# A mixture-of-experts stage: from pairs of experts with 64 sorted slots to fours of experts with 32 tokens each

## The reference

```python
group_p = softmax(xt @ w_group);  group_w, group_id = top_k(group_p, 1)
in_group = (xt @ w_router) restricted to that group
top_logits, local_id = top_k(in_group, 2)
gates = group_w * softmax(top_logits)
# per expert e, over its tokens:
h = silu(xb @ w_gate[e]) * (xb @ w_up[e]);  y_e = h @ w_down[e]
y[token] += gate * y_e          # two experts per token
```

## Time and profile before

| | |
|---|---|
| time, median of three runs | 3320.39 us |
| the profiled execution's span | 3318.3 us |
| PE busy | 2797.8 us (84%) |
| DVE, ACT busy | 855.7, 472.3 us |
| read from HBM | 777.00 MB, mean 235 GB/s |
| experts, block 1, each of two layers | 237.3 us from first product to last combine |
| experts, block 2, each of two layers | 465.6 us |
| routing, each of four layers | 36.5 to 38.3 us |

### The profile page before, as it was taken

How to read it: one execution, slowest core, us unless ns; L and a number is a source line. 1 busy time by engine, 2 the same in 40 slices (tenths; PEclk the granted TensorE clock), 3 DMA queues, 4 the chain that set the end, 5 groups by cost and what they waited for, 6 DMA issues and landing times. The chain is left out here.

```text
span 3318.3 us, 34187 instructions
## 1 busy us (share of the span) xinstructions
PE 2797.8 (84%) x13108; PEld 1699.9 (51%) x13108; DVE 855.7 (26%) x1849; ACT 472.3 (14%) x879; POOL 0.2 (0%) x4
## 2 busy tenths in 40 slices
PE   6869997868996994869898889869858797988886
PEld 4544445544443852858743333347547686333333
DVE  1442221343122126351121111111364312110111
ACT  1311110321111002200111011010121001101111
POOL 0000000000000000000000000000000000000000
PEclk9889998888998997969989999989978798999998
DMA  6015995114994553003349999864700032899994
GB/s 266 32 54 215 428 419 217 51 46 166 427 428 189 236 192 163 1 1 129 150 191 429 428 429 428 374 276 166 289 1 1 26 152 105 368 429 429 428 429 206
DMA packets 55690, 779.39 MB, mean 235 GB/s; under 512 B 6825, under 2 KB 7081, under 8 KB 7849
## 3 DMA queue, kind: packets, MB, share of 16 engines
q1 hardware_dynamic: 55592, 778.07, 56.4%
HBM read 777.00 MB, written 1.05 MB: 234 GB/s over the span
## 5 line engine op out<-in xcount | busy, mean ns | idle before, releaser
L1657 PE MATMUL bank<-ring,arena 128*64 128x512 f32 x3072 | 703.6, 612 | 84.6 <-issue 70.1
L1657 PEld LDWEIGHTS bank<-ring,arena 128*64 128x64 f32 x3072 | 240.8, 141 | 538.7 <-issue 538.4
L1684 PE MATMUL bank<-ring,arena 128*64 128x512 f32 x1536 | 343.7, 596 | 0.0
L1639 PE MATMUL bank<-arena 128*128 128x256 f32 x1088 | 263.5, 386 | 3.6 <-DVE arena L1740 3.6
L1639 PEld LDWEIGHTS bank<-arena 128*128 128x128 f32 x1088 | 196.1, 190 | 80.2 <-issue 58.9
L1727 DVE TENSOR_TENSOR arena<-bank,arena 128x256 f32<-128x256 f32 (+1 forms) x64 | 35.7, 558 | 776.6 <-ACT arena L1704 776.6
L825 PE MATMUL bank<-xnT,ring 128*128 128x256 f32 x960 | 211.4, 383 | 9.3 <-PEq L271 9.3
L1684 PEld LDWEIGHTS bank<-ring,arena 128*64 128x64 f32 x1536 | 104.6, 137 | 193.5 <-issue 193.5
L825 PEld LDWEIGHTS bank<-xnT,ring 128*128 128x128 f32 x960 | 184.6, 193 | 35.9 <-issue 10.3
L1357 PE MATMUL bank<-xnT,ring 128*128 128x256 f32 x768 | 177.1, 384 | 23.8 <-PEq L962 23.8
L1357 PEld LDWEIGHTS bank<-xnT,ring 128*128 128x128 f32 x768 | 148.1, 193 | 46.1 <-issue 25.4
(11 more groups left out here) (335 smaller groups left out, 2822.9 us busy)
## 6 DMA issues: line engine op xcount, KB each, us to landing
ring<-in_w_exp SPq DMA_DIRECT2D x288, 2048.0 KB, 15.5
ring<-in_w_ada SPq DMA_DIRECT2D x24, 2048.0 KB, 7.9
ring<-in_w_in SPq DMA_DIRECT2D x20, 2048.0 KB, 11.3
ring<-in_w_merge SPq DMA_DIRECT2D x18, 2048.0 KB, 17.1
ring<-in_w_o SPq DMA_DIRECT2D x8, 2048.0 KB, 16.4
ring<-in_w_conv SPq DMA_DIRECT2D x6, 2048.0 KB, 27.5
ring<-in_w_rest SPq DMA_DIRECT2D x2, 1696.0 KB, 21.1
small<-in_small SPq DMA_DIRECT2D x2, 1440.0 KB, 22.9
```

The lines of the kernel that those rows point to most:

```text
L1639: nc.tensor.matmul(bank[d // 2][:, T * (d % 2):T * (d % 2) + T], Yw[:, P * d:P * d + P], gwT, start=False, stop=False, skip_group_check=True)
L1657: last = nc.tensor.matmul(o[rows(e), 0:MW], Xw[:, k, WIN * e:WIN * e + WIN], ring[:, slot(n), MW * k:MW * k + MW], start=k == 0, stop=k == ...
L1684: last = nc.tensor.matmul(o[rows(e), :], hidT[:, j, WIN * e:WIN * e + WIN], ring[:, slot(n), at:at + MW], start=j == 0, stop=j == ft - 1)
```

## The change

`route` and `experts` become one function, `moe`. The experts run four at a time (a "quad", `QUAD` = 4, eight a layer), with 32 tokens each (`WIN` = 32). If an expert of a quad has more than 32 tokens, the quad runs again for the next 32 with the same weights; such a run of a quad is an "item". There is no sort by slot and no `Xs`: before each item DVE compares the ranks with 1 to 32 and makes `onehot` (tokens x 4 x 32), and PE gathers the item's tokens with it, 16 products of 128 columns, into banks 6 and 7; ACT and DVE copy them to `Xw`. The same `onehot` times the gates gives `gw`. The gather for the next item stands behind the combine of the previous one. Four experts write 32 partitions of the result bank each. Small tables in `offs`, made by DVE, say which quad and which round an item is. SP's loop becomes a written-out list of loads which waits for those tables. The final sum of each bank is released by itself, so DVE's additions start before the last combine. The `slots` table and its load are gone.

```diff
-        WIN = 64
+        WIN = 32
+        QUAD = 4
+        NQ = NE // QUAD
         ROUNDS = T // WIN
...
                 def _(sp):
-                    sp.dma_start(iota, dram["slots"]).then_inc(slots_in, 16)
+                    sp.wait_ge(tables_ready, 1)
+                    for q in range(NQ):
+                        if q:
+                            earlier = sp.value_load(offs[0:1, LAST_AT + q - 1:LAST_AT + q], min_val=0, max_val=ITEMS * per_turn)
...
+                        for n in range(RING if q == 0 else 0, per_turn):
+                            if n < RING:
+                                sp.wait_ge(w_used, earlier + (n0 + n + per_turn - RING + 1))
+                            else:
+                                sp.wait_ge(w_used, same + (n0 + n - RING + 1))
+                            sp.dma_start(ring[:, slot(n), :], feed(q, n)).then_inc(w_loaded[slot(n)], 16)
...
+                    for b in range(4):
+                        nc.tensor.matmul(bank[b][:, :], K("zeros"), cst[:, 0:512], start=True, stop=False, skip_group_check=True)
...
-                    pe.wait_ge(once_ready, TT)
-                    for d in range(KT):
+                    def gather():
+                        for d in range(KT):
+                            for t in range(TT):
+                                last = nc.tensor.matmul(gather_banks[d // 4][:, P * (d % 4):P * (d % 4) + P], xtok[:, t, P * d:P * d + P], onehot[:, t, :],
+                                                        start=t == 0, stop=t == TT - 1)
+                            if d == 3:
+                                last.then_inc(low_gathered, 1)
+                        last.then_inc(high_gathered, 1)
...
+                    pe.wait_ge(onehot_ready, 1)
+                    gather()
+                    pe.wait_ge(tables_ready, 1)
+
+                    def item(it, more):
...
+                        pe.wait_ge(low_taken, it + 1)
+                        pe.wait_ge(high_taken, it + 1)
+                        pe.wait_ge(y1_taken, it + 1)
+                        for o, first in ((gate_bank, 0),) if shared else ((gate_bank, 0), (up_bank, QUAD)):
+                            if first:
+                                pe.wait_ge(y0_taken, it + 1)
+                            for e in range(QUAD):
+                                here(first + e)
+                            for k in range(KT):
+                                for e in range(QUAD):
+                                    last = nc.tensor.matmul(o[rows(e), :], Xw[:, k, rows(e)], ring[:, slot(first + e), MW * k:MW * k + MW],
+                                                            start=k == 0, stop=k == KT - 1)
+                                    if k == KT - 1:
+                                        last.then_inc(w_used, 1)
+                        pe.wait_ge(y0_taken, it + 1)
+                        pe.wait_ge(gwT_ready, it + 1)
+                        combine()
+                        if more:
+                            pe.wait_ge(onehot_ready, it + 2)
+                            gather()
+                        pe.wait_ge(hid_made, it + 1)
+                        for j in range(ft):
+                            last = nc.tensor.transpose(gate_bank[:, P * j:P * j + P], hid[:, P * j:P * j + P], K("ident"))
+                        last.then_inc(hid_turned, 1)
+                        pe.wait_ge(gw_ready, it + 1)
                         for t in range(TT):
...
+                        pe.wait_ge(hidT_ready, it + 1)
+                        for n in range(n_gu, per_turn):
+                            here(n)
+                        for half, o in ((1, y1_bank), (0, y0_bank)):
+                            if half == 0:
+                                pe.wait_ge(gwT_ready, it + 2)
+                            for j in range(ft):
+                                for e in range(QUAD):
+                                    n, at = (n_gu + e // 2, ft * D * (e % 2)) if shared else (n_gu + e, 0)
+                                    at += D * j + MW * half
+                                    last = nc.tensor.matmul(o[rows(e), :], hidT[:, j, rows(e)], ring[:, slot(n), at:at + MW], start=j == 0, stop=j == ft - 1)
...
-                    then(nc.vector.tensor_tensor_scan(cum, K("ones")[:, 0:NE], count, 0.0, ALU.mult, ALU.add))
-                    then(nc.vector.tensor_tensor(first, cum, count, ALU.subtract))
...
-                        then(nc.vector.tensor_scalar(once[:, t, :], iota, lo[:, t, :], None, ALU.is_equal))
-                        nc.vector.scalar_tensor_tensor(once[:, t, :], iota, hi[:, t, :], once[:, t, :], ALU.is_equal, ALU.add).then_inc(once_ready, 1)
...
+                    dve.wait_ge(high_gathered, 1)
+                    take_high()
+
+                    dve.wait_ge(y0_taken, 1)
+                    then(nc.vector.tensor_reduce(most, count.rearrange("p (q e) -> p q e", e=QUAD), AX, ALU.max))
...
+                    then(nc.vector.scalar_tensor_tensor(offs[:, RANK_AT:RANK_AT + ITEMS + 1], before_it, float(NE * TT), quad_of, ALU.mult, ALU.add))
+                    nc.vector.memset(spare[:, 1:2], 0.0).then_inc(tables_ready, 1)
...
-                    dve.wait_ge(sum_ready, 1)
                     for d in range(KT):
+                        dve.wait_ge(sum_ready, d // 2 + 1)
```

## The result

The changed kernel takes 3421.48 us, the median of four runs (3419.43 to 3431.85), against 3320.42 us for the kernel before beside it: a ratio of 1.0307, 95% interval 1.0292 to 1.0322. Its profiled execution has a span of 3417.6 us, 99.3 more than before, and a mean granted clock of 0.832.

A forecast was written before the change was run, and what follows sets the result against it. PE bounds block 1's experts, loads block 2's. Span 3318.3 - 24 (block 2 without ring losses) - 16 (block 1) + 141 (ring losses) = 3419.3 us, 3421 for the runs; range 3310 to 3480.

The forecast's parts named there:

- Part 1: Routing, ahead of the experts: first expert product 9 us earlier in each of four layers, bounds 6 to 11.
- Part 2: Experts' products: four experts on 32 columns run together, 64 instructions in 7.1 us, so both blocks become load-bound.
- rival 3: Experts' products: fours don't run four at once; bursts 14.2 us (time 3710) or 8.9 us (3522); chance 0.05.
- Part 3: Ring of expert chunks: runs dry as four slots return at once; 42 losses of 2.6 us, 14 of 2.3, 141 us.
- the signs: What would show each step, here in block 2's experts: about 370 GB/s, not 405, gate groups 66 us apart.
- burst - 6.5: Ring of expert chunks: us lost per group given back, if above zero; 0.6 at a burst of 7.1 us.
- Rival 2: Ring losses are larger: bursts stay low 6 us and more, 3.5 to 4 us a group, 3475 to 3505; chance 0.08.
- Rival 1: Ring: slack of two chunks in flight is enough; loss 0 to 0.6 us a group, 3281 to 3315; chance 0.17.
- Part 4: Experts' stages: first burst 2 us more, block 2's end 5.0 less; block 1's second layer repeats its first quad, +20.

The follow-up runs named there:

- x1: Changed kernel with each expert chunk loaded as two halves, first halves given back before the burst's end (gate and up: halfway): 3287.57 us.
- x2: Changed kernel with each expert chunk loaded as two halves, both given back only after the group's last product: 3422.36 us.
- x3: Changed kernel with PE kept busy by zero products ahead of gate, up and down groups in block 2 and gate groups in block 1: 3347.84 us.
- x4: Changed kernel with gate and up groups made longer by 16 products whose result is overwritten: 3584.39 us.
- x5_before_halves: Kernel before the change with the experts' chunks loaded as two halves, nothing else changed: 3329.41 us.
- x9: Changed kernel with early-released halves (block 2: first two chunks of four), zero products behind the first gather and ahead of block 2's groups: 3269.32 us.
- x8: Changed kernel with the gather in the loop done twice, the second overwriting the first: 3403.54 us.

## Why the prediction was right, step by step

**Part 1** said 9 us a layer; the table shows 9.6 to 9.8. The steps, in the changed kernel's timeline, where the earlier trace rows had a gather of 15.97 us and a clearing of 3.67 on the way:

```profile
248.84 3.60 PE L1519 MATMUL bank<-cst 128*128 128x512 f32 x8
...
254.33 3.84 PE L1535 MATMUL bank<-arena 128*128 128x128 f32 x32 [0.85 <-DVE arena L1654]
...
258.81 0.18 DVE L1706 TENSOR_REDUCE arena<-arena 128x8 f32<-128x32 f32 x1
...
263.43 0.06 DVE L1725 MEMSET spare<- 128x1 f32 x1
...
265.81 8.76 PE L1567 MATMUL bank<-ring,arena 128*32 128x512 f32 x64 [7.65 <-issue]
```

The gather is 3.84 us (3.9 said). DVE's tables take 4.7 us (5.2 said), and from their end to the first product pass 2.3 us (1.6 said, between 0.5 and 4).

**Part 2** holds: 64 instructions on 32 columns take 7.05 to 7.07 us in a busy stretch (rival 3 said 8.9 or 14.2). The Trainium skill's 2.38 for three column tiles (TensorE: Matmul & The Clock Gate, Part 3) had pointed to a lower gain than this kernel has: four column tiles here do 64 instructions in the time in which two of 64 columns do 32. The clearing products take 3.60 us for 8 instructions of the same 512 columns one after another, so 64 would take 28.8 us (an estimate), four times as long.

**Part 3** is where nearly all of the time is, and its two sizes hold: losses of 2.6 and 2.3 us a group were said, 2.66 is the mean over block 2, and bursts of 9.1 and 8.8 us, 9.26 in the mean (behind waits of 12.6 us and more ahead of gate and up groups, where about 10 were said). A mean interval is made of the burst, 9.26, then 0.14 us to the issue, 7.82 to the first landing, 4.87 to the next one, and 0.14 to the first product. Block 2's experts were to be 52 us longer in each layer (15 losses of 2.6, 7 of 2.3, less 3 for the first burst and the end) and are 56.9 and 55.5. Its gate groups stand 66.7 us apart, as said (66); the 358 GB/s are under the "about 370" of the signs, where 52 us more would themselves make 364 (405 x 465.6 / 517.6). x1 against x2 shows that the loss hangs on the release, x3 and x4 that it hangs on the burst. The term is a little off at its low end: "burst - 6.5" gives 0.6 at a burst of 7.07 us, and x3 shows 1.3 there. Rival 2 (3.5 to 4 us a group) lies above the mean of 2.66. Rival 1 (slack enough) would thus have needed more than a short burst: x3, in which 33 of 46 bursts are short, is still slower than the kernel before by 0.84%. The estimate by the Trainium skill's formula for one DMA (DMA: Bandwidth & Descriptors, Anatomy of one DMA), 1.1 us less a group and 3360 us, doesn't hold for these loads, which SyncE issues and not GpSimd: the same 2 MB load's 7.9 us from issue to landing, 7.82 in the interval above, was the figure to use, not 6.8. About a microsecond of that restart, from the issue at 1724.18 to the bytes in the slice from 1725, is the end of the hole that the windows show.

**Part 4.** The first bursts take 8.6 to 8.9 us after about 7.5 us of idling, where 9.1 was said. Block 2's end, which the earlier trace rows had at 19.0 us after the last down chunk, and the second round in the second layer of block 1:

```profile
2205.26 8.42 PE L1595 MATMUL bank<-ring,arena 128*32 128x512 f32 x64 [8.55 <-DMA ring<-in_w_exp]
...
2214.66 3.69 PE L1543 MATMUL bank<-arena 128*128 128x256 f32 x16 [0.98 <-DVE arena L1749]
2215.80 3.47 DVE L1761 SCALAR_TENSOR_TENSOR hT<-bank,mod,hT 128x256 f32<-128x256 f32 x8 [1.29 <-PE bank L1543]
```

```profile
771.29 8.61 PE L1567 MATMUL bank<-ring,arena 128*32 128x512 f32 x64 [7.44 <-issue]
...
791.26 7.05 PE L1567 MATMUL bank<-ring,arena 128*32 128x512 f32 x64
```

From 2205.26 to 2219.27 are 14.0 us, as said, and the first quad's second run starts 20.0 us after its first, as said. Its cost is 17.8 us (264.0 less 246.2, the two layers having been equal before), not 20. Block 1 as a whole: with six losses of 2.6 us a layer the prediction had +6.6 and +26.6 for its experts, measured +5.2 and +22.9. These terms, 5 us too high, and Part 1, 3 us too high, offset Part 3, 8 us too low in block 2. That the sum came within 2 us of the span (3419.3 against 3417.6) is partly that.

There is luck of another kind in the comparison. The first router product is 5.0 us earlier than before (238.6 against 243.6), and that isn't the change. x5_before_halves, which is the kernel before up to there, has it at 238.1, and x1_halves_early, with the change, at 243.9; each of the eleven profiled executions has it between 237.9 and 238.9 or between 243.5 and 243.9. The difference arises in the attention: from 115 to 130 us the granted clock was 1.00 in all of the former and 0.54 to 0.58 in all of the latter. So 5 us of the difference between the two spans are of the executions and not of the kernels, and the "rest" of -2.5 us in the table holds them; later stretches give half of it back.

## What to carry to other kernels

With a ring of slots, count how many chunks are in flight when the largest group is given back. The transfer time of these and of the next chunk (here 14.7 us) must cover the group's burst at the clock that PE has after its wait, and the time from the release to the landing of the next load (here about 8 us, that chunk's transfer included). Take that as the least: at a burst of 7.07 us the loss was 0.7 us more. Making the compute faster in larger groups can lose time, as here: PE waited longer for chunks, its bursts began at half the clock, and slots were given back later. The cure is cheap: release parts of a group as they are used, and put harmless products ahead of the burst where the loads set the pace.

## What the runs showed of the hardware that was not expected

- More work on PE made kernels faster: the second gather by 18 us (3403.5 against 3421.5), zero products by 74 us (3347.8), and by 14 us on top of the early release.
- How slow a burst begins isn't ordered by the wait ahead of it: after 12.8 us of waiting one takes 9.95 us, another, in x1, 8.54 after 9.99, one 9.40 after only 4.3, and near 2.2 us both 8.77 and 7.07 are found in x9.
- Loads of 1 MB in rows of 8 KB run at 422 GB/s where loads of 2 MB in rows of 16 KB run at 428.
- A load issued while the stream still ran took longer to land than one issued as it ran dry: 8.63 us against 7.82 (x3's 33 short bursts, the changed kernel's 46 bursts); 8.90 behind the 14 short bursts of x8.
- The same code ran 5 us shorter or longer in the attention from one execution to the next, with the granted clock at 1.00 or at 0.54 to 0.58 from 115 to 130 us.
